# Rotary embeddings in a two-block transformer kernel: rotated halves fetched by small DMAs between partitions in place of permutation products

## The reference, cut to what matters

```python
def rotary(x, pos, rot_dim, base):
    half = rot_dim // 2
    inv = jnp.exp(-math.log(base) * jnp.arange(half, dtype=jnp.float32) * 2.0 / rot_dim)
    ang = pos.astype(jnp.float32)[..., None] * inv
    cos, sin = jnp.cos(ang)[:, :, None, :], jnp.sin(ang)[:, :, None, :]
    x1, x2 = xf[..., :half], xf[..., half:rot_dim]
    return jnp.concatenate([x1 * cos - x2 * sin, x1 * sin + x2 * cos, xf[..., rot_dim:]], axis=-1)
```

## Time and profile before

| | us |
|---|---|
| median of three runs | 2101.42 (2099.67 to 2102.14) |
| profiled execution, its own time | 2098.33 |
| span of that execution | 2096.2 |
| TensorE busy (matmul) | 2011.9, 96% of the span |
| VectorE busy | 935.7, 45% |
| ScalarE busy | 731.6, 35% |
| GpSimd busy | 787.5, 38% |
| mean granted clock of TensorE | 0.981 of full speed |

### The profile page before, as it was taken

One profiled execution on the slowest core, in us unless ns is written; L12 is line 12 of the kernel. 1 busy time (PEld: TensorE's weight loads), 2 busy tenths in 40 slices (PEclk: granted clock), 3 DMA queues, 4 the chain that ended last, 5 costly groups with the idle time before them and its releaser, 6 DMA issues.

```text
span 2096.2 us, 25921 instructions
## 1 busy us (share of the span) xinstructions
PE 2011.9 (96%) x9460; PEld 1580.7 (75%) x9460; DVE 935.7 (45%) x1500; ACT 731.6 (35%) x1213; POOL 787.5 (38%) x333
## 2 busy tenths in 40 slices
PE   6999899999999999999899999997899999999999
PEld 5778455588878888888688888774566888888887
DVE  5763655433752453456562105677872333111111
ACT  4233445533431242343223224525344333222221
POOL 3364321144444344434444443230022433444442
PEclk8999999999999999999999999999799999999999
DMA  6345021134757466536533343230021433343431
GB/s 164 91 116 136 20 56 36 35 91 113 197 159 204 121 181 182 146 94 182 143 102 81 100 110 71 51 81 21 21 59 43 100 96 81 96 104 87 101 99 61
DMA packets 156614, 211.16 MB, mean 101 GB/s; under 512 B 15432, under 2 KB 133736, under 8 KB 156392
## 3 DMA queue, kind: packets, MB, share of 16 engines
q1 hardware_dynamic: 140672, 166.37, 32.1%
q10 hardware_dynamic: 15848, 43.51, 6.9%
HBM read 206.69 MB, written 2.10 MB: 100 GB/s over the span
## 4 chain that ended last, share of the span: by engine, by line
issue 55%; PE 22%; POOL 20%; ACT 1%; DVE 1%; ACTq 0%; POOLq 0%; DVEq 0%
POOL wlo L541 20%; PE ps L577 7%; PE ps L579 7%; PE ps L578 7%; DVE xT L2173 0%; DVE st L1807 0%; POOL rkT L559 0%; POOL rkT L556 0%; POOLq L545 0%; DVE hlo L1801 0%; POOLq L536 0%; PE ps L620 0%; POOL retlo L561 0%; PE ps L632 0%; ACT xrow L1762 0%
## 5 line engine op out<-in xcount | busy, mean ns | idle before, releaser
L541 POOL TENSOR_TENSOR wlo<-raw,whi 128x1024 fp32r<-128x1024 f32 (+1 forms) x317 | 772.2, 2452 | 1249.8 <-ACT whi L1272 1221.1
L577 PE MATMUL ps<-hhi,whi 128*128 128x512 f32 x1488 | 593.8, 399 | 5.3 <-DVE hlo L1801 3.0
L579 PE MATMUL ps<-hhi,wlo 128*128 128x512 f32 x1488 | 582.9, 392 | 0.0
L578 PE MATMUL ps<-hlo,whi 128*128 128x512 f32 x1488 | 582.5, 391 | 0.0
L1272 ACT ACTIVATE whi<-raw 128x1024 fp32r<-128x1024 f32 x309 | 316.3, 1053 | 401.3 <-PE ps L579 375.4
L577 PEld LDWEIGHTS ps<-hhi,whi 128*128 128x128 f32 x1488 | 281.5, 189 | 75.9 <-issue 17.8
L579 PEld LDWEIGHTS ps<-hhi,wlo 128*128 128x128 f32 x1488 | 281.1, 189 | 60.0
L578 PEld LDWEIGHTS ps<-hlo,whi 128*128 128x128 f32 x1488 | 281.5, 189 | 56.9 <-issue 1.4
L577 PE MATMUL ps<-hidhi,whi 128*128 (+1 forms) x608 | 236.9, 390 | 3.0 <-DVE mod L2200 3.0
L578 PE MATMUL ps<-hidlo,whi 128*128 (+1 forms) x608 | 236.6, 389 | 0.0
L579 PE MATMUL ps<-hidhi,wlo 128*128 (+1 forms) x608 | 236.5, 389 | 0.0
(11 more groups left out here) (374 smaller groups left out, 2462.5 us busy)
## 6 DMA issues: line engine op xcount, KB each, us to landing
raw<-in_ffn_w SPq DMA_DIRECT2D x264, 256.0 KB, 3.8
raw<-in_w_in SPq DMA_DIRECT2D x154, 256.0 KB, 4.0
trig<-in_ada_w ACTq DMA_DIRECT2D x72, 512.0 KB, 4.5
raw<-in_w_up SPq DMA_DIRECT2D x64, 256.0 KB, 4.0
raw<-in_w_down SPq DMA_DIRECT2D x64, 256.0 KB, 4.1
raw<-in_w_out SPq DMA_DIRECT2D x32, 256.0 KB, 3.9
xrow<-in_x ACTq DMA_DIRECT2D x4, 512.0 KB, 6.6
raw<-in_cmp_k_w SPq DMA_DIRECT2D x8, 256.0 KB, 3.7
```

What stands on the lines that cost most here:

```text
L541: last = pool.tensor_tensor(lo, src, hi.bitcast(F32), ALU.subtract)
L577: pe.matmul(out_, lhi, rhi, start=first, stop=False)
L578: pe.matmul(out_, lhi, rlo, start=False, stop=False)
L579: return pe.matmul(out_, llo, rhi, start=False, stop=last)
```

## The change

The permutation matrices and their products go. ScalarE issues, for each chunk to be rotated, DMAs from `st` to a ring of buffers (four for nsa, rq and rk, two in `tmp` for dsa) that put each half of the rotated dimensions where the other half stands: for a width of 64 four DMAs of 8 partitions, for 128 two of 64, for 32 eight of 4; 28 in nsa, 8 in rq, 8 in rk, 44 in dsa, 88 in all. The sign is put into the sine table by the scale of ScalarE's sine. The product with the cosine is taken from the chunk's PSUM bank (for chunks without a norm), by VectorE, and counted in `pj_cos`; the next user of that bank waits for it. VectorE clears the buffers before it makes the tables. Core of the diff:

```diff
+C_PN, C_PR, C_PI = range(3)
+ROTATED = {C_PN: (64, 16), C_PR: (128, 128), C_PI: (32, 8)}
@@ tensor: projection
                 def bank(x):
                     if x >= 4:
                         pe.wait_ge(pj_ev, x - 3)
+                    if x - 4 in COS:
+                        pe.wait_ge(pj_cos, COS[x - 4])
...
                     for kind, v in turns[n]:
-                        c = chunks[v]
-                        if p >= 4:
-                            pe.wait_ge(pj_dve, p - 3)
                         if kind == "ms":
                             pe.wait_ge(pj_ev, out_of[v] + 1)
                             m = post_ms(name, v)
-                            pe.matmul(ps[:, 4 + p % 4, :], cst[:, C_HD64:C_HD64 + P], SQ[m % 4], start=True, stop=True)\
+                            if m >= 4:
+                                pe.wait_ge(pj_root, m - 3)
+                            pe.matmul(ps[:, 4 + m % 4, :], cst[:, C_HD64:C_HD64 + P], SQ[m % 4], start=True, stop=True)\
                               .then_inc(pj_post, 1)
-                        else:
...
-                            pe.matmul(ps[:, 4 + p % 4, :], cst[:, perm:perm + P], st[:, v % 4, :], start=True, stop=True)\
-                              .then_inc(pj_post, 1)
@@ tensor: compress_hidden
                 pe.wait_ge(pj_ev, GEND[("rq", "rk")[kv]])
+                pe.wait_ge(pj_cos, COS_END[("rq", "rk")[kv]])
@@ scalar
+            def fetch_halves(name, v, kind):
+                width, rot = ROTATED[kind]
+                at, dst = ROT_SLOT[name, v]
+                sc.wait_ge(rot_clear, 1)
+                if ROT_FREE[name, v]:
+                    sc.wait_ge(pj_dve, ROT_FREE[name, v])
+                for h in range(P // width):
+                    for a, b in ((0, rot // 2), (rot // 2, 0)):
+                        r0 = h * width
+                        sc.dma_start(dst[r0 + a:r0 + a + rot // 2], st[r0 + b:r0 + b + rot // 2, v % 4, :])\
+                          .then_inc(rot_landed[at], 16)
@@ scalar: projection
+                    for kind, u in turns[n]:
+                        if kind == "perm" and chunks[u][0] == "normrope":
+                            sc.wait_ge(pj_dve, post_event[name, "ms", u] + 1)
+                            fetch_halves(name, u, chunks[u][5])
                     if n < len(BL[name]):
...
                                 a.then_inc(pj_ev, 1)
+                                copied[v] = g
+                                if c[0] == "rope" and name != "dsa":
+                                    sc.wait_ge(pj_ev, g + 1)
+                                    fetch_halves(name, v, c[4])
...
+                        elif chunks[u][0] == "rope" and name == "dsa":
+                            sc.wait_ge(pj_ev, copied[u] + 1)
+                            fetch_halves(name, u, chunks[u][4])
@@ vector: trig_tables
                 link(ve.tensor_copy(posf, posi[:, :]))
+                if b == 0:
+                    ve.memset(Pb[:, :, :], 0.0)
+                    ve.memset(PT[:, :, :], 0.0).then_inc(rot_clear, 1)
@@ vector: projection
+                def rotate(v):
...
+                    if c[0] == "normrope":
+                        link(ve.tensor_tensor(dst, st[:, v % 4, :], trig[:, tb, 0, :], ALU.mult))
+                    ve.wait_ge(rot_landed[at], ROT_LANDED[name, v])
+                    link(ve.tensor_tensor(r, r, trig[:, tb, 1, :], ALU.mult))
+                    ve.tensor_tensor(dst, dst, r, ALU.add).then_inc(pj_dve, 1)
...
                     for kind, v in turns[n]:
...
-                            link(ve.tensor_tensor(tmp[:, 0, :], st[:, v % 4, :], trig[:, tb, 0, :], ALU.mult))
-                            link(ve.tensor_tensor(tmp[:, 1, :], ps[:, 4 + p % 4, :], trig[:, tb, 1, :], ALU.mult))
-                            ve.tensor_tensor(BUF[c[1]][:, c[2], :], tmp[:, 0, :], tmp[:, 1, :], ALU.add)\
-                              .then_inc(pj_dve, 1)
+                            if c[0] == "normrope":
+                                ve.wait_ge(pj_dve, post_event[name, "ms", v] + 1)
+                            else:
+                                ve.wait_ge(pj_cos, COS_OF[name, v])
+                            rotate(v)
+                    if n < len(BL[name]):
+                        b = BL[name][n]
+                        for c, ch in enumerate(b[4] if b[0] in "BK" else ()):
...
+                            elif ch[0] == "rope":
                                 ve.wait_ge(trig_ready, table_base + 4)
+                                ve.wait_ge(pj_ev, x + 1)
+                                ve.scalar_tensor_tensor(out=BUF[ch[1]][:, ch[2], :], in0=ps[:, x % 4, :],
+                                                        scalar=ch[5], in1=trig[:, ch[3], 0, :],
+                                                        op0=ALU.mult, op1=ALU.mult).then_inc(pj_cos, 1)
```

More of the change, by code:

```diff
@@ L44 @@
 CMP_S = 16
-C_ID, C_MEAN, C_HD128, C_HD64, C_PN, C_PR, C_PI, C_CAUSAL, C_ADM, C_CMP, C_MISC = [i * P for i in range(11)]
+C_ID, C_MEAN, C_HD128, C_HD64, C_CAUSAL, C_ADM, C_CMP, C_MISC = [i * P for i in range(8)]
 C_AV = C_MISC
@@ L269, in mix_kernel @@
                                                                              "pj_dve", "pj_silu"))
+        rot_clear, pj_cos = sem("rot_clear"), sem("pj_cos")
+        rot_landed = [sem(f"rot_landed{i}") for i in range(6)]
         rt_qk, rt_sd, rt_pv, rt_ev, rt_sum, rt_root, rt_rcp, rt_m, rt_o, rt_hi, rt_done = (
@@ L320, in mix_kernel @@
         post_ms = lambda name, v: n_ms[name, v]
+        ROT_SLOT, ROT_LANDED, ROT_FREE = {}, {}, {}
+        landed, taken, ropes = {}, {}, {}
+        for name in BL:
+            ring = [SQ[0], SQ[1], SQ[2], SQ[3]] if name in ("nsa", "rq", "rk") else [tmp[:, 0, :], tmp[:, 1, :]]
+            kind_of = "sq" if len(ring) == 4 else "tmp"
+            for turn in PLAN[name][1]:
+                for kind, v in turn:
+                    if kind == "perm":
+                        c = PLAN[name][0][v]
+                        slot = ropes.get(kind_of, 0) % len(ring)
+                        ropes[kind_of] = ropes.get(kind_of, 0) + 1
+                        at = slot if kind_of == "sq" else 4 + slot
+                        width, rot = ROTATED[c[4] if c[0] == "rope" else c[5]]
+                        landed[at] = landed.get(at, 0) + 16 * 2 * (P // width)
+                        ROT_SLOT[name, v] = (at, ring[slot])
+                        ROT_LANDED[name, v] = landed[at]
+                        ROT_FREE[name, v] = taken.get(at, 0)
+                        taken[at] = post_event[name, "perm", v] + 1
+        COS, COS_OF, COS_END = {}, {}, {}
+        n_cos = 0
+        for name, blocks in BL.items():
+            g, v = G0[name], 0
+            for b in blocks:
+                for c, ch in enumerate(b[4] if b[0] in "BK" else ()):
+                    if ch[0] == "rope":
+                        n_cos += 1
+                        COS[g + n_out[b[0]] - len(b[4]) + c] = COS_OF[name, v] = n_cos
+                    v += ch[0] in ("rope", "norm", "normrope")
+                g += n_out[b[0]]
+            COS_END[name] = n_cos
         N_ROW_DMAS = 13
@@ L1347, in projection @@
                 s = AT[name]
-                g, v, x, root, silu, p = G0[name], 0, 0, R0[name], SL0[name], P0[name]
+                g, v, root, silu, copied = G0[name], 0, R0[name], SL0[name], {}
                 msq = R0[name]
@@ L2351, in constants @@
     c[:, C_HD64:C_HD64 + P] = (r[:, None] // 64 == r[None, :] // 64) / 64.0
-    for at, width, rot in ((C_PN, 64, 16), (C_PR, 128, 128), (C_PI, 32, 8)):
-        half = rot // 2
-        for m in range(P):
-            d = m % width
-            if d < half:
-                c[m + half, at + m] = -1.0
-            elif d < rot:
-                c[m - half, at + m] = 1.0
+    for kind, (width, rot) in ROTATED.items():
+        c[:, C_SIGN + kind] = np.where(r % width < rot // 2, -1.0, 1.0)
     c[:, C_CAUSAL:C_CAUSAL + P] = np.where(r[None, :] <= r[:, None], 0.0, NEG)
```

55 lines of the change are left out of this document (24 added, 31 removed).

## The result

The changed kernel takes 2138.45 us (median of 4 runs, 2135.65 to 2139.29), the kernel before 2101.67 in the same comparison: slower, ratio 1.0175, 95% interval [1.0162, 1.0189]. The forecast was 2131, its range 2116 to 2145.

What follows compares the result with a forecast made beforehand. TensorE, busy 96% of the span, was taken as the bound, so new waits on it are losses. First projection 17.0, rq and rk 2.0 and last projection 10.3 sum to +29.3 us, giving 2131 for the median, range 2116 to 2145.

Steps and rivals of the forecast that it cites:

- nsa, +17.0: First projection: 17.8 us waiting for cosine products behind the tables, 2.6 for the lowered clock, less 3.4 for removed products.
- the issues themselves cost nothing in this part: First projection: ScalarE's copies, highs and eight issues take 8 us of a 10.9 us block, so fetch issues add nothing.
- No change: Start of nsa's row block: 1.9 us from the previous block's end, about the 0.94 + 0.86 of today.
- rq and rk, +2.0: Blocks behind the two compressions: issues ahead of ScalarE's highs delay GpSimd's splits, +1.0 us each, range 0 to 2.8.
- dsa's row block, +11.6: Last projection: block waits for index-query cosine products behind VectorE's reciprocals, starting at 1400.7 instead of 1389.09.
- VectorE's last rotation, landed at 1426.6, is just covered: End of dsa: ScalarE's last copies, done at 1428.0, set attention's start; dsa stage +10.3 us in all.
- Other stages keep their instructions: Everything outside the first projection, rq and rk, and dsa, attention included: no term added to the sum.
- The products, -3.4 and -3.4: Removed permutation products at 0.86 us each: four in the first projection and four in dsa gain 3.4 us each.
- rival (d): Not slower: cosine products found done at the third block's start, products gained against rq and rk's 2.0; 2095, chance 0.04.
- (a): Rival: fetch issues on ScalarE cost next to nothing, 4.8 us less than forecast; 2126, chance 0.05.
- (b): Rival: fetch issues are dear, 1.5 us each, 32 us in the last projection and 7 elsewhere; about 2170, chance 0.07.
- (c): Rival: index-query cosine products don't hold dsa's row block, as the copy chain moves up; 11.6 go, 2119, chance 0.08.

Runs made afterwards that it cites:

- e_nsa_st: Changed kernel with nsa's cosine products read from ScalarE's SBUF copy instead of the PSUM banks, fetches kept: 2121.21 us, ratio 1.0096 to the kernel before.
- e_nofetch: Changed kernel without fetches, leaving out the exchange of halves; cosine products read the SBUF copy in all four projections: 2104.32 us, ratio 1.0003 to the kernel before.
- e_warm: Changed kernel with 76 products whose result nothing reads, run by TensorE in nsa's 18.5 us wait: 2137.73 us, ratio 1.0177 to the kernel before.
- e_both: Changed kernel with cosine products from the SBUF copy in all four projections and dsa's last 16 fetches issued early: 2116.59 us, ratio 1.0083 to the kernel before.
- e_late: Changed kernel with the fetches of nsa, rq and rk issued behind ScalarE's splits of the next weights: 2133.59 us, ratio 1.0164 to the kernel before.
- e_best: e_both plus e_late's order, and half of the buffers cleared in VectorE's idle time before the tables: 2115.14 us, ratio 1.0072 to the kernel before.
- e_best2: e_best with dsa's last 16 fetches left where the change has them: 2112.06 us, ratio 1.0049 to the kernel before.
- e_dsa_st: Changed kernel with cosine products read from the SBUF copy in dsa alone: 2128.45 us, ratio 1.0125 to the kernel before.
- e_order: Changed kernel with dsa's index-query cosine products moved ahead of VectorE's second pair of reciprocals, still reading the banks: 2124.89 us, ratio 1.0113 to the kernel before.
- e_early: Changed kernel with dsa's last 16 fetches issued before ScalarE's copies of the row block: 2125.91 us, ratio 1.0128 to the kernel before.
- e_fill: Changed kernel with 18 products whose result nothing reads, run by TensorE ahead of its wait for dsa's last rotation: 2137.89 us, ratio 1.019 to the kernel before.

## Why the prediction was right, and where its steps failed

Slower, by 1.75%, inside the range; the main mechanism held at both places. Point by point:

- **nsa, +17.0: measured +17.1.** The wait was predicted to end at 68.85 and ended at 68.01: the cast of the positions took 0.41 us instead of 1.59 (by chance: it is 1.58 again in e_nsa_st and e_nofetch) and the four long steps of VectorE came back as assumed. The clock was put at 2.6, all behind the wait; by e_warm it is 1.4 there and as much again in the row block, 2.9 by its end: nearly right in sum, in two places. By e_nsa_st 3.2 of the 17.1 are there without any wait at the banks: "the issues themselves cost nothing in this part" held only because the longer wait hid them. "No change" at the row block's start held (17.36 later there).
- **rq and rk, +2.0: measured +3.0.** The cause isn't shown. The same stretch is -0.1 in e_nofetch, without fetches, and +2.7 in e_both, with them and without cosine products from the banks, which speaks for the fetches; but e_late, which puts them behind ScalarE's highs, has +2.9 too, and e_best and e_best2, with one and the same program there, have +0.2 and +3.7. I gave back 0.3 of each 1.2 to 1.4 for VectorE's earlier rotations; the rows show 1.5 each, with nothing given back.
- **dsa's row block, +11.6: measured +10.7** against the section's start. e_dsa_st and e_order both take it away, 10.2 and 9.6 of it against the same start.
- **"VectorE's last rotation, landed at 1426.6, is just covered": this step failed.** I let ScalarE's last copies set attention's start. The landing was right to 0.3 us (25.6 us behind the row block's start, against the forecast 25.9), but I took 0.7 for each of the two steps behind it, in a place where GpSimd's slabs had just begun: they took 2.8 and 2.7. Attention's first product is 31.3 us behind the row block's start, not 27.3. With the row block 0.9 early that makes the 3.0 between +10.3 and the measured +13.3. TensorE's wait for pj_dve in forget_keys should have been listed as a term.
- **Attention, 0: measured +6.1. This step, "Other stages keep their instructions", failed too.** The instructions are the same and the stage is longer. e_early takes all of it away and e_fill nothing, which looks like a price of the late last rotation; but e_late and e_warm keep that wait and have 4.4 and 4.6 us less. The time is lost where the granted clock is low, 0.67 over the first 30 us against 0.89 before; the forecast had a clock term behind nsa's wait and none here, and what lowers the grant isn't settled. The whole miss against 37.4 is 8.1 us: 0.1, 1.0, 3.0 and 6.1 of these points, less the 2.2 that the stages between gave back, all to a tenth. That the time is inside the range all the same is in part luck: the upper bound allows for further long steps of VectorE, which the last rotation had, but none of its terms is a slower attention.
- **The products, -3.4 and -3.4:** they do leave TensorE's queue, with less than 3.4 in dsa: the four at 1402.15 had 3.04 us to the next block's start, so 0.86 for each was too much there, and the way from that row block's start to the next block's is 1.3 us shorter (16.1 to 14.8). e_nofetch shows that in nsa, rq and rk the gain lasts only as long as a larger wait hides what stands behind; in dsa it is 3.6 us. In rival (d), "not slower, 2095", ten of them were counted as gains once the waits are gone; with all waits and fetches gone the time is 2104. That rival's price was 9 us too good in the median; 5.1 of it were nsa's products, which give nothing, and the 3.4 of dsa come out as 3.6 over all eight.
- **The rivals.** (a), issues at next to nothing: an issue is 0.61 to 0.63 us, as the earlier trace rows had it, and 16 in a row are 10.0 us, which e_early and e_both show on TensorE's path. The rule of the Trainium skill ("DMA: Bandwidth & Descriptors", section "Issuing engines are not separate DMA queues"), that this time is usually small beside the DMA, is not borne out by these fetches: the last of the 16 issues starts at 1441.3 and its data is used at 1443.31, so 0.6 of 2.0 us are the issue, and 16 issues stand in a row. (b) falls by the same rows. (c) falls: the row block was held.

## What to carry to other kernels

A producer's "done" that is moved from a fast reader (a copy by ScalarE) to a busy one (VectorE's product) makes that reader's whole queue part of the producer's path: list what stands ahead of it in the queue, at every place where the buffer is reused. Work removed from the busiest engine is worth nothing where the block behind it waits for another engine (nsa, rq and rk here; in dsa 3.6 us of it came through): before counting it, find what ends the next wait, and whether it moves too. And many small DMAs on a computing engine's queue are work of that engine, at 0.6 us each here, and where they stand in its order counts: the move of 16 of them that gained 12.5 us alone (e_early) made TensorE wait 9.4 us once the block ahead of them came sooner (e_both). Last, a gain read from one trace of each kernel needs a second look where it is under some 5 us: two kernels that are the same up to a place were 4.2 us apart there.

## What the runs showed of the hardware that I had not expected

- VectorE's small steps suffer most beside GpSimd's slabs: a cast of 128x128 took 2.36 us there and 0.22 alone, a product of 128x512 2.79 and 0.69, the pair of hidlo steps 4.73 and 2.34. The cast and the product each lose 2.1 us, whatever the size, and four such steps in a row took the 10 us of the four slabs beside them.
- The issue time of a fetch doesn't grow with its size: for 8 and 16 KB (dsa) it is 608 ns in the median, for 16 KB (nsa) 632, for 128 KB (rq and rk) 468 to 621.
- The granted clock fell to 0.63 in attention right behind 30 us in which TensorE was busy 28.4 of them at 0.94 (e_fill), and stayed at 0.94 in e_early with the same instructions and fewer busy us (21.6 of 30). What sets it there was not found.
- Dummy products do hold the clock where they fill an idle stretch: 1.00 instead of 0.80 between 50 and 100 us in e_warm.
